# The gated delta rule cut into two phases, with the innermost blocks of its inverse computed on VectorE

## The reference

```python
qkv = silu(causal_dwconv(concatenate([q, k, v]), gdn_conv_w))          # 4 taps
q = l2_normalize(q) * 128 ** -0.5;  k = l2_normalize(k)                # 8 heads of 128
beta = sigmoid(b_a);  g = -exp(a_log) * softplus(a_a + dt_bias)
# per head, in chunks:  gc = cumsum(g)
decay = exp(where(causal, gc[i] - gc[j], -inf))
lmat = where(strict, (k * beta) @ k.T * decay, 0) + eye
sol = triangular_solve(lmat, [v * beta, k * beta * exp(gc)])           # u, w
qk = q @ k.T * decay;  q_dec = q * exp(gc);  k_dec = k * exp(gc[-1] - gc)
# step over the chunks:
v_new = u - w @ state
o = q_dec @ state + qk @ v_new
state = state * exp(gc[-1]) + k_dec.T @ v_new
o_a = rms_norm(o, gdn_norm_w) * silu(z_a)
```

## Time and profile before

| | |
|---|---|
| median of 3 runs | 2433.18 us (2431.31 to 2436.58) |
| the profiled execution | 2434.0 us, its span 2432.2 us |
| mean granted TensorE clock | 0.981 of full speed |
| TensorE matmuls busy | 2307.3 us, 95% of the span, 10652 records |
| VectorE, ScalarE, GpSimd busy | 48%, 39%, 17% |
| chain of work that ended last | TensorE 85%, ScalarE 6%, VectorE 4% |
| DMA | 177 MB, mean 73 GB/s |

### The profile page before, as it was taken

One profiled execution on the slowest core, in us unless ns is written; L12 is line 12 of the kernel. 1 busy time (PEld: TensorE's weight loads), 2 busy tenths in 40 slices (PEclk: granted clock), 3 DMA queues, 4 the chain that ended last, 5 costly groups with the idle time before them and its releaser, 6 DMA issues.

```text
span 2432.2 us, 29410 instructions
## 1 busy us (share of the span) xinstructions
PE 2307.3 (95%) x10652; PEld 1835.6 (75%) x10652; DVE 1163.9 (48%) x1476; ACT 941.8 (39%) x1374; POOL 407.5 (17%) x327
## 2 busy tenths in 40 slices
PE   7899999989898999999899999999999988999999
PEld 4777777777776788877666678888877856788887
DVE  3444444456544566622532256664235435566622
ACT  4444444434243444422355544443133233444421
POOL 1233333221200122200120012221000001222200
PEclk9999999999999999999999999999999998999999
DMA  4111111111122233322111123333212212233322
GB/s 145 36 44 34 35 43 34 44 44 56 58 78 78 76 96 95 111 95 72 68 50 29 35 78 97 95 103 107 92 61 87 78 35 78 78 95 95 113 94 70
DMA packets 46302, 177.13 MB, mean 73 GB/s; under 512 B 5136, under 2 KB 5136, under 8 KB 46224
## 3 DMA queue, kind: packets, MB, share of 16 engines
q1 hardware_dynamic: 46224, 176.06, 22.7%
HBM read 173.94 MB, written 2.10 MB: 72 GB/s over the span
## 4 chain that ended last, share of the span: by engine, by line
PE 85%; ACT 6%; DVE 4%; issue 2%; POOL 1%; DMA 0%; ACTq 0%; DVEq 0%; SPq 0%; POOLq 0%
PE acc L245 20%; PE acc L247 20%; PE acc L246 20%; PE bank L1459 3%; PE bank L1452 2%; PE bank L1002 1%; PE acc L1947 1%; PE acc L1945 1%; PE acc L1946 1%; ACT whi L182 1%; PE bank L221 1%; PE bank L1026 1%; PE bank L222 1%; PE bank L223 1%; PE bank L320 1%
## 5 line engine op out<-in xcount | busy, mean ns | idle before, releaser
L245 PE MATMUL acc<-HH,whi 128*128 128x512 f32 x1688 | 684.4, 405 | 24.8 <-POOL HL L337 18.0
L247 PE MATMUL acc<-HH,wlo 128*128 128x512 f32 x1688 | 662.8, 393 | 0.0
L246 PE MATMUL acc<-HL,whi 128*128 128x512 f32 x1688 | 662.4, 392 | 0.0
L182 ACT ACTIVATE whi<-raw 128x1024 fp32r<-128x1024 f32 (+1 forms) x296 | 327.8, 1108 | 748.3 <-PE acc L247 717.0
L188 DVE TENSOR_TENSOR wlo<-raw,whi 128x1024 fp32r<-128x1024 f32 (+1 forms) x296 | 410.9, 1388 | 386.1 <-ACT whi L182 386.1
L245 PEld LDWEIGHTS acc<-HH,whi 128*128 128x128 f32 x1688 | 319.8, 189 | 102.8 <-POOL HL L337 18.1
L247 PEld LDWEIGHTS acc<-HH,wlo 128*128 128x128 f32 x1688 | 319.5, 189 | 68.7
L246 PEld LDWEIGHTS acc<-HL,whi 128*128 128x128 f32 x1688 | 320.1, 190 | 63.0 <-issue 3.4
L245 PE MATMUL acc<-FH,whi 128*128 128x512 f32 x528 | 211.3, 400 | 0.0
L247 PE MATMUL acc<-FH,wlo 128*128 128x512 f32 x528 | 208.5, 395 | 0.0
L246 PE MATMUL acc<-FL,whi 128*128 128x512 f32 x528 | 208.5, 395 | 0.0
(11 more groups left out here) (341 smaller groups left out, 2908.4 us busy)
## 6 DMA issues: line engine op xcount, KB each, us to landing
raw<-w SPq DMA_DIRECT2D x258, 512.0 KB, 3.6
raw<-w SPq DMA_DIRECT2D x48, 704.0 KB, 4.1
X<-x SPq DMA_DIRECT2D x4, 512.0 KB, 7.6
out<-X SPq DMA_DIRECT2D x8, 256.0 KB, 5.4
cst<-cst SPq DMA_DIRECT2D x1, 960.0 KB, 5.1
small<-small SPq DMA_DIRECT2D x1, 512.0 KB, 4.4
par<-par SPq DMA_DIRECT2D x1, 457.0 KB, 5.8
```

Of the source, the lines that this page charges most:

```text
L182: nc.scalar.activation(hi[:, 0:kt * P], raw[u % RAW][:, 0:kt * P], ACT.Copy).then_inc(w_hi_ready, 1)
L245: nc.tensor.matmul(a[:, :], wh, tile(hi, k), start=start and k == 0, stop=False)
L246: nc.tensor.matmul(a[:, :], wh, tile(lo, k), start=False, stop=False)
L247: last = nc.tensor.matmul(a[:, :], wl, tile(hi, k), start=False, stop=stop and k == kt - 1)
```

## The change

The stage is split into two phases, unrolled over the heads.

**First phase** (`prep_*`), 8 heads, two units each (q and k): taps, silu, norms, prefix sums, K K^T, Q K^T; per head it keeps A (`AM`), the decayed scores (`QK`), decayed q (`QD`) and normalised k (`KN`) in SBUF. One exponential serves both decays: |difference| instead of two clipped ones.

**Inverse of the 32-blocks.** A is stored to DRAM (`store_a`) and read back so that one partition holds one 32 x 32 block: 16 blocks a head, 4 heads a batch, 64 partitions (`l_blk`). VectorE inverts them by columns, 31 steps of a product and a difference (`inverse_dve`), then a transposing copy. The inverse and its transpose go to DRAM (`spread`) onto zeros written before (16 stores behind unit 6's load), and each head's `l_xt` and `l_x` are loaded from there. Batch A is computed in the first phase (steps 0 to 3 at the end of head 4, the rest in heads 5, 6, 7), batch B in heads 0 and 1 of the second.

**Second phase** (`heads_*`), 8 heads, two units each (v of the next head, z of the next; in the last head ssd units): only levels 5 and 6 of the inverse remain on TensorE, those of head h + 1 between the chunks of head h. Every DMA is issued by SP, in one list with the weights (`load_l1`). Masks 0 to 4 and the transpose of mask 0 are gone.

`load_xt(h)` waits for the last new value of head h - 3, whose buffer it takes, `load_x(h)` for the last level of head h - 1. `decayed_dve` forms A and the scores of a head (four products of 128 columns and one of 512). In `heads_dve`, `xt` and `x` are the updates of the two levels, `vb` and `kd` the products of v with beta and of k with its decay.

The core of the diff (the new functions, cut; the removed ones are those of the section above):

```diff
+        def inverse_dve(dve, batch, j0, j1):
+            n, rows, base = 16 * FIRST_BATCH, slice(0, 16 * FIRST_BATCH), 63 * batch
+            a = l_blk[rows, :].rearrange("p (i j) -> p i j", j=32)
+            x = l_inv[rows, :].rearrange("p (i j) -> p i j", j=32)
...
+            for j in range(j0, j1):
+                m = 31 - j
+                t = l_tmp[rows, 0:m * (j + 1)].rearrange("p (i c) -> p i c", c=j + 1)
+                if j:
+                    dve.wait_ge(c_inv, base + 2 * j)
+                nc.vector.tensor_tensor(t, a[:, j + 1:32, j:j + 1].to_broadcast([n, m, j + 1]),
+                                        x[:, j:j + 1, 0:j + 1].to_broadcast([n, m, j + 1]), ALU.mult).then_inc(c_inv, 1)
+                dve.wait_ge(c_inv, base + 2 * j + 1)
+                nc.vector.tensor_tensor(x[:, j + 1:32, 0:j + 1], x[:, j + 1:32, 0:j + 1], t, ALU.subtract).then_inc(c_inv, 1)
+            if j1 == 31:
+                dve.wait_ge(c_inv, base + 62)
+                nc.vector.tensor_copy(a, x.rearrange("p i j -> p j i")).then_inc(c_inv, 1)
+        INVERSE_A = {5: (0, 4), 6: (4, 13), 7: (13, 22), 8: (22, 31)}
+        INVERSE_B = {0: ((0, 4), (4, 8), (8, 12)), 1: ((12, 18), (18, 24), (24, 31))}

+        def prep_dve(dve, c):
...
+            for h in range(1, NH + 1):
+                p = h - 1
+                for b in (1, 2, 3):
+                    tap_dve(dve, c, k_conv(p), b)
+                split_lo(dve, u0 + 2 + 2 * h, None, 0, KD)
...
+                else:
+                    decayed_dve(dve, p - 1)
+                if h in INVERSE_A and h > 5:
+                    inverse_dve(dve, 0, *INVERSE_A[h])
+                for b in (1, 2, 3):
+                    tap_dve(dve, c, q_conv(h) if h < NH else v_conv(0), b)
+                split_lo(dve, u0 + 3 + 2 * h, None, 0, KD)
+                dve.wait_ge(s_rs, 2 * p + 1)
...
+                nc.vector.scalar_tensor_tensor(out=l_qn[:, :], in0=conv_q[p % 2][:, :], scalar=P ** -0.5, in1=l_rs[0][:, :],
+                                               op0=ALU.mult, op1=ALU.mult).then_inc(c_n, 1)
+                dve.wait_ge(s_rs, 2 * p + 2)
+                nc.vector.tensor_tensor(tile(KN, p), conv_k[p % 2][:, :], l_rs[1][:, :], ALU.mult).then_inc(c_n, 1)
+                if h == 5:
+                    inverse_dve(dve, 0, *INVERSE_A[h])

+        def prep_pe(pe, c):
...
+            for h in range(1, NH + 1):
+                p = h - 1
+                unit(1 + 2 * h)
...
+                for k in range(2):
+                    pe.wait_ge(s_sq, 2 * p + k + 1)
+                    nc.tensor.matmul(bank[k][:, :], ones, l_sq[k][:, :], start=True, stop=True).then_inc(p_sum, 1)
+                unit(2 + 2 * h, 0)
+                unit(2 + 2 * h, 1)
...
+                four(bank[2], l_gb, upper).then_inc(p_prod, 1)
+                unit(2 + 2 * h, 2)
+                unit(2 + 2 * h, 3)
+                pe.wait_ge(c_n, 2 * p + 2)
...
+                four(bank[3], tile(KN, p), tile(KN, p)).then_inc(p_prod, 1)
+                four(bank[4], tile(KN, p), l_qn).then_inc(p_prod, 1)

+            def level_yt(h, l):
+                pe.wait_ge(g_m, 2 * h + l - 4)
+                if l == 5:
+                    pe.wait_ge(xt_in[h % 3], 16 * (h // 3 + 1))
+                    pe.wait_ge(c_kd, h if h else 1)
+                else:
+                    pe.wait_ge(c_xt, 2 * h + 1)
+                    pe.wait_ge(s_yt, 2 * h + 1)
+                four(bank[4], l_m, l_xt[h % 3]).then_inc(p_yt, 1)

+        def heads_pe(pe, c):
...
+            unit(19, 0)
+            turn_k(0)
+            unit(19, 1)
+            turn_v(0)
+            level_yt(0, 5)
+            unit(19, 2)
+            level_xy(0, 5)
+            unit(19, 3)
+            level_yt(0, 6)
+            level_xy(0, 6)
+            for h in range(NH):
+                more, a, b = h < NH - 1, 20 + 2 * h, 21 + 2 * h
+                new_values(h, 0)
+                unit(a, 0)
+                outputs(h, 0)
+                if more:
+                    level_yt(h + 1, 5)
+                old_values(h, 1)
+                unit(a, 1)
+                new_values(h, 1)
+                unit(a, 2)
+                outputs(h, 1)
+                if more:
+                    level_xy(h + 1, 5)
+                old_values(h, 2)
+                unit(a, 3)
+                new_values(h, 2)
+                unit(b, 0)
+                outputs(h, 2)
+                if more:
+                    level_yt(h + 1, 6)
+                    turn_v(h + 1)
+                old_values(h, 3)
+                unit(b, 1)
+                new_values(h, 3)
+                unit(b, 2)
+                outputs(h, 3)
+                if more:
+                    level_xy(h + 1, 6)
+                    turn_k(h + 1)
+                unit(b, 3)
...
+                nc.tensor.matmul(bank[3][:, :], ones, l_t[:, :], start=True, stop=True).then_inc(p_osum, 1)

+        def heads_dve(dve, c):
...
+            for h in range(NH):
+                more = h < NH - 1
+                cv = v_conv(h + 1) if more else s_conv(0)
+                state(h, 0)
+                tap_dve(dve, c, cv, 1)
+                if h:
+                    normed(h - 1)
+                rest(h, 1)
+                tap_dve(dve, c, cv, 2)
+                split_lo(dve, u0 + 21 + 2 * h, None, 0, KD)
+                state(h, 1)
+                tap_dve(dve, c, cv, 3)
+                if more:
+                    xt(h + 1, 5)
+                rest(h, 2)
+                if more:
+                    x(h + 1)
+                if h in INVERSE_B:
+                    inverse_dve(dve, 1, *INVERSE_B[h][0])
+                state(h, 2)
+                rest(h, 3)
+                if more:
+                    vb(h + 1)
+                else:
+                    for b in (1, 2, 3):
+                        tap_dve(dve, c, s_conv(1), b)
+                split_lo(dve, u0 + 22 + 2 * h, None, 0, KD)
+                if h in INVERSE_B:
+                    inverse_dve(dve, 1, *INVERSE_B[h][1])
+                if more:
+                    xt(h + 1, 6)
+                    kd(h + 1)
+                if h in INVERSE_B:
+                    inverse_dve(dve, 1, *INVERSE_B[h][2])

+        def load_l1(sp, c):
...
+            def spread(batch):
+                sp.wait_ge(c_inv, 63 * (batch + 1))
+                sp.wait_ge(z_filled, 32 * NH)
+                for j in range(FIRST_BATCH):
+                    h, rows = FIRST_BATCH * batch + j, slice(16 * j, 16 * j + 16)
+                    sp.dma_start(dram_blocks(xt_dram, h), l_blk[rows, :]).then_inc(x_spread, 16)
+                    sp.dma_start(dram_blocks(x_dram, h), l_inv[rows, :]).then_inc(x_spread, 16)
+                sp.wait_ge(x_spread, 32 * FIRST_BATCH * (batch + 1))
...
+            for n, k in enumerate(place_of):
+                u = c["u"] + n
+                if u >= RAW:
+                    sp.wait_ge(w_lo_ready, u - RAW + 1)
...
+                if n == 6:
+                    for t in (x_dram, xt_dram):
+                        for h in range(NH):
+                            sp.dma_start(dram_head(t, h), l_inv[:, 0:S].rearrange("p (c n) -> p c n", c=NC)).then_inc(z_filled, 16)
+                if n in (10, 12, 14, 16):
+                    store_a((n - 10) // 2)
+                if n == 22:
+                    spread(0)
+                    load_xt(0)
+                    load_x(0)
+                    load_xt(1)
+                    load_xt(2)
+                    for h in range(FIRST_BATCH, NH - 1):
+                        store_a(h)
+                if n == 24:
+                    store_a(NH - 1)
+                if n in range(24, 37, 2):
+                    h = (n - 24) // 2
+                    load_x(h + 1)
+                    if h == 1:
+                        spread(1)
+                    if h + 3 < NH:
+                        load_xt(h + 3)
```

More of the change, by code:

```diff
@@ new lines, in four, with unit @@
+        def four(out, lhs, rhs):
+            for k in range(NC):
+                last = nc.tensor.matmul(chunk(out, k), chunk(lhs, k), rhs if rhs is upper else chunk(rhs, k), start=True, stop=True)
+            return last
+        def prep_pe(pe, c):
+            def unit(n, part=None):
+                multiply(pe, c["u"] + n, c["t"] + n, None, 0, 0, KD, HH, HL, part=part)
+            multiply(pe, c["u"], c["t"], None, 0, 0, KD, HH, HL, ready=(h_ready, c["h"] - KD))
+            unit(1)
+            tables_pe(pe, c)
+            unit(2)
+            chunk_sums_pe(pe)
+            for h in range(1, NH + 1):
+                p = h - 1
+                unit(1 + 2 * h)
+                if p == 0:
+                    pe.wait_ge(a_steps, 8)
+                for k in range(2):
[3 more added lines that the diff above has]
+                unit(2 + 2 * h, 1)
+                pe.wait_ge(g_gb, p + 1)
+                if p:
+                    pe.wait_ge(s_egb, p)
+                four(bank[2], l_gb, upper).then_inc(p_prod, 1)
```

(48 more changed lines are left out.)

716 lines of the change are left out of this document (403 added, 313 removed).

## The result

The changed kernel takes 2314.5 us (median of 4 runs, 2314.1 to 2317.0), the kernel before on the same chip 2432.2 us; the ratio is 0.952, with a 95% interval of 0.951 to 0.953. The forecast was 2317.

A forecast was written before the change was run, and what follows sets the result against it. TensorE, busy 95% of the span, was taken as the bound. Savings of 130.7 us less new costs of 17.6 gave net 113, 2434 to 2321 us; 4 more off for the cross-check made 2317, range 2297 to 2346.

The forecast's parts named there:

- Levels and mask 0 off TensorE: Delta rule stage: inverse levels 1 to 4 and mask 0's transpose leave TensorE, 11.7 us per head, 93.5 us in eight.
- Waits removed: TensorE's waits in the delta rule stage, 38.2 us, go except 1 us in the last head: 37.2 us saved.
- the prologue: Head 0's last level has nothing to hide its copy and update: a new cost of 1.6 us.
- The gross saving: Work and waits off TensorE: 130.7 us; counting the new heads from below (15.7 and 22.0 us) gave 139.
- VectorE's price: Inverse on VectorE: 24.3 us per batch, from 0.14 us fixed, 1.09 ns an element and 0.04 us handover.
- A stall costs clock too: One or two new TensorE stalls reach 3 us and lower the granted clock: 2 us, bounds 0 and 5.
- Stores of A and batch B: Way through DRAM: some 13 us and a head ahead of their readers, so hidden, at no cost.
- Zeros and batch A's way back: DRAM way: zeros take 15 us with 28 us of room, batch A out and back 10 us; both hidden.
- The small-piece rival: DMA pieces cost 0.08 us each, making zeros and batch A's spread late by 29 us: 2346 us; chance 0.12.
- the slower case: DMA piece price eats the 117 us gain from 0.194 us; at 0.25 us, 2477 us; chance 0.04.
- ScalarE as the bound: Rival: ScalarE bounds the first phase, 1 us in each half head, 16 us: 2332 us; chance 0.07.
- VectorE slower: Rival: inverse operations 0.2 us dearer, from small patterns or GpSimd beside them: 2340 us; chance 0.18.

The follow-up runs named there:

- run 3: Changed kernel with the load of x of head 3 ahead of batch B's spread and both inverse batches' 62 VectorE steps left out; ratio 0.9391, 2284.6 us.
- Run 1: Changed kernel with only the load of x of head 3 moved ahead of batch B's spread in SP's list; ratio 0.9477, 2307.6 us.
- run 10: Changed kernel with 16 more stores of zeros, to DRAM nobody reads, behind the first 16; ratio 0.953, 2319.6 us.
- run 9: Batch A in seven pieces instead of four, against a version with batch B over three heads and loads reordered (2299.5 us); ratio 0.9498, 2309.2 us.
- run 4: Changed kernel with the load of x of head 3 moved ahead of the spread and batch A's steps alone left out; ratio 0.9437, 2296.5 us.

## Why the prediction was right, and where it was not

**Levels and mask 0 off TensorE (93.5 us):** right. 81.9 measured for the levels, 84.9 of it as work (2.65 us each where I had 2.70, so 86.4); the transposes' 7 us are from the rows and were not measured alone.

**Waits removed (37.2 us):** right. Idle time falls from 47.6 to 10.5 us between the kernel before and run 3, by 37.1. Run 3's 10.5 us contain 2 us of short waits at head 0's levels and the first of head 1's, the prologue among them, so slightly more than I had counted is gone.

**The gross saving (130.7, cross-check 139) was too small.** It is 521.11 - 371.58 = 149.5 us, with the prologue and ScalarE's share already taken off. I went on with the lower count "which stands on rows alone" and gave back half of the difference. The head counts from below were the better ones, and still high: 15.7 against 15.37 and 22.0 against 21.03, together 1.3 us per head or 10 in eight. Even the higher count left 10 us unseen.

**VectorE's price (24.3 us per batch):** right, 24.5 and 23.8. The reason given for it was not quite: the first piece of batch A lies beside all three of GpSimd's operations, and its steps there took 3.5 us instead of about 0.8. Its stalls: batch A was given 2.9 + 2.5 + 1.7 = 7 us in three waits and had 4.3 + 2.9 = 7.2 in two; behind the middle piece no wait came (that head took 15.37 us). So the sum is right and its division is not. Batch B was given 5.5 + 0.5, measured 2.4 + 0.6 + 3.7 = 6.7, in head 1, where it was said to be.

**"A stall costs clock too: 2 us (0 to 5)":** the size was wrong and outside its bounds, the mechanism right. TensorE's same work took 12.3 us more busy time in the changed kernel than in run 3. I had priced one or two stalls of 3 us by the one in the earlier trace rows; there were four of 2.4 to 4.3 us and the late load, all but the shortest followed by work at the lower level. Even two waits of 0.7 and 0.5 us in head 0 of the second phase had 0.50 behind them (198 to 200 us). A: 10.6 us for 7.2 of waits; B: 11.6 for 6.7; SP's list: 12.4 for 8.8.

**"Stores of A and batch B ... Hidden":** this step failed: put at nothing, it cost 12.4 us. I had asked what SP's wait for `p_vn` holds back, and not what stands behind SP's wait for the end of batch B. The stores themselves are early enough; the load of x of head 3 behind them is not. Run 1 shows it by moving that one load.

**Zeros and batch A's way back: hidden**, as predicted. A piece costs 0.032 us at 512 B and 0.015 at 128 B, against my 0.03 and 0.015; doubled, the zeros overrun their room by 3.6 us (run 10), where 28 us of room and 2 x 15 of work gave 2. The load that ran out of room beside unit 7 was x of head 1. The first `level_yt` did not wait: xt was issued at 182.0 after a spread that began at 174.7. The small-piece rival (0.08 us) and the slower case (0.194) are out. The read-modify-write rule of the Trainium skill (DMA: Bandwidth & Descriptors, Specifications) says that 128 B pieces are off line rate, and the trace agrees in that: a quarter of the bytes costs half of the price. Whether read-modify-write is the reason, no run shows. And 256 x 0.015 = 3.8 us for the spread is far from the rival's 20.

**ScalarE as the bound:** out. First-phase heads follow each other at 15.37 us with no wait for it. **VectorE slower:** out as a whole, but true beside GpSimd; run 9 shows what it costs when pieces are put there.

**Balance:** gross 149.5; on the same footing I had 130.7 + 4 less the prologue's 1.6 and ScalarE's 1, 132.1. New costs 34.5; on the same footing 7 + 6 + 2 = 15. The two errors, 17 and 20 us, cancelled to within 2 at the mark, and 4 us more came in later stages. The step that took back the most was the load behind SP's wait. That the sum is right is luck to this extent.

## What to carry to other kernels

A list of DMAs on one engine's queue is a path of its own: for each wait in it, write down everything that stands behind and when its reader comes, and put a load that doesn't need the wait ahead of it. Moving one load was worth 0.4%, and each relocation showed the next load in the list. Of a stall on TensorE price the idle time and the lower clock behind it; here the second was about half of the first in sum (12.3 us for 22.3), but for a single wait it ran from nothing (2.4 us) to 2.9 us (behind 4.3, from the granted clock of 143.6 to 150 us). VectorE took work well only where GpSimd was idle too, so place by timeline and not by share.

## What the runs showed of the hardware that was not expected

A VectorE step on 64 partitions took 1.22 to 1.35 us instead of 0.24 to 0.38 beside a GpSimd operation of 1.3 to 1.4 us: VectorE seems to wait for GpSimd's operation to end instead of sharing with it. 64x87 and 64x220 both came to about the same length, and the step of 1.26 us above ended at 124.71, 0.1 us after GpSimd's (124.61). That is read from the times; no run moved GpSimd's operation alone.

And the length of a wait did not decide on the clock behind it. In run 4, behind one of 2.39 us, the granted clock was 0.72 from 226 to 232 us; in the changed kernel, behind the same wait of 2.40 us, it was 1.00 from 235.9 to 242, and in run 10 behind one of 2.8 us 1.00 too.
